# Twelve adaLN modulation products in groups of four weight slots, nine groups of them issued in the first mixer

## The reference

```python
cs = jax.nn.silu(c)                                   # (1, 1024)
for i in range(DEPTH):                                # 2 layers
    mod = (cs @ ada_w[i] + ada_b[i])[:, None, :]      # 1024 x 6144 weights each
    sh1, sc1, gt1, sh2, sc2, gt2 = jnp.split(mod, 6, axis=-1)
    h = rmsnorm_2(x, norm_w[i, 0]) * (1.0 + sc1) + sh1
    ...
```

## Time and profile before

| | us |
|---|---|
| median of 3 runs | 3378.33 (3377.92 to 3379.85) |
| the profiled execution | 3374.32 |
| its span, first to last instruction | 3372.4 |
| TensorE busy | 3001.6 |
| DVE busy | 1308.4 |
| ACT busy | 1030.4 |
| POOL busy | 243.7 |

### The profile page before, as it was taken

One profiled execution on the slowest core, in us unless ns is written; L12 is line 12 of the kernel. 1 busy time (PEld: TensorE's weight loads), 2 busy tenths in 40 slices (PEclk: granted clock), 3 DMA queues, 4 the chain that ended last, 5 costly groups with the idle time before them and its releaser, 6 DMA issues.

```text
span 3372.4 us, 44139 instructions
## 1 busy us (share of the span) xinstructions
PE 3001.6 (89%) x18608; PEld 2286.4 (68%) x18608; DVE 1308.4 (39%) x2098; ACT 1030.4 (31%) x1734; POOL 243.7 (7%) x189
## 2 busy tenths in 40 slices
PE   8989579989887888789898999999796879999998
PEld 6878467878675777668786656565595766656564
DVE  5563466555455334355463111111284541111111
ACT  5443335454443221254443111111253241111111
POOL 1000001010001223110010000000102300000000
PEclk9999699999997999889998999999897979999999
DMA  7423015445234552045343799999450036999994
GB/s 317 188 96 138 25 70 198 183 159 188 90 138 175 212 188 76 13 175 187 110 153 151 306 379 367 380 367 379 191 178 10 14 125 258 367 379 369 377 370 200
DMA packets 95539, 695.31 MB, mean 206 GB/s; under 512 B 10592, under 2 KB 10720, under 8 KB 11232
## 3 DMA queue, kind: packets, MB, share of 16 engines
q1 hardware_dynamic: 95328, 692.32, 52.5%
HBM read 691.23 MB, written 1.05 MB: 205 GB/s over the span
## 4 chain that ended last, share of the span: by engine, by line
PE 83%; DVE 8%; ACT 5%; issue 3%; POOL 1%; DMA 0%; ACTq 0%; SPq 0%; DVEq 0%; POOLq 0%
PE bank L1451 13%; PE bank L714 11%; PE bank L716 11%; PE bank L715 11%; PE bank L1498 7%; PE bank L1514 7%; PE bank L1429 4%; PE bank L1733 2%; PE bank L1741 2%; PE bank L1745 1%; PE bank L2193 1%; PE bank L1845 1%; PE bank L543 1%; PE bank L1307 1%; PE bank L1328 1%
## 5 line engine op out<-in xcount | busy, mean ns | idle before, releaser
L1451 PE MATMUL bank<-weight_ring,packed_h 128*64 128x256 f32 x2176 | 285.4, 379 | 0.0
L714 PE MATMUL bank<-source_hi_lo,weight_hi_lo 128*128 128x256 f32 x864 | 256.0, 296 | 28.3 <-DVE source_hi_lo L704 11.9
L1507 DVE COPY down<-bank 128x512 f32<-128x512 f32 x128 | 88.5, 692 | 475.2 <-PE bank L1498 475.2
L1451 PE MATMUL bank<-more_slots,packed_h 128*64 128x256 f32 x1920 | 257.0, 379 | 1.5 <-ACT packed_h L1438 1.5
L714 PE MATMUL bank<-gate_up_hi_lo,x_hi_lo 128*128 128x512 f32 x640 | 253.9, 397 | 0.0
L715 PE MATMUL bank<-source_hi_lo,weight_hi_lo 128*128 128x256 f32 x864 | 250.2, 290 | 0.0
L716 PE MATMUL bank<-source_hi_lo,weight_hi_lo 128*128 128x256 f32 x864 | 250.1, 289 | 0.0
L716 PE MATMUL bank<-gate_up_hi_lo,x_hi_lo 128*128 128x512 f32 x640 | 249.7, 390 | 0.0
L715 PE MATMUL bank<-gate_up_hi_lo,x_hi_lo 128*128 128x512 f32 x640 | 249.1, 389 | 0.0
L1451 PEld LDWEIGHTS bank<-weight_ring,packed_h 128*64 128x64 f32 x2176 | 196.2, 137 | 74.4 <-issue 18.1
L1514 PE MATMUL bank<-down,hidden_and_scatter_T 128*128 128x512 f32 x512 | 233.8, 599 | 1.6 <-DVE down L1507 1.6
(11 more groups left out here) (520 smaller groups left out, 5527.9 us busy)
## 6 DMA issues: line engine op xcount, KB each, us to landing
weight_ring<-weight_slots SPq DMA_DIRECT2D x443, 1024.0 KB, 6.2
more_slots<-weight_slots SPq DMA_DIRECT2D x212, 1024.0 KB, 7.8
params_sb<-small_params SPq DMA_DIRECT2D x1, 3215.0 KB, 17.9
x_sb<-x_T SPq DMA_DIRECT2D x1, 1024.0 KB, 5.0
out_T<-x_sb SPq DMA_DIRECT2D x4, 256.0 KB, 2.1
params_sb<-small_params SPq DMA_DIRECT2D x1, 73.5 KB, 4.8
```

Source lines behind the costliest of these rows:

```text
L714: e.matmul(out, w[0], x[0], start=start, stop=False, skip_group_check=shared)
L1451: mm = e.matmul(ps[x * CAP:(x + 1) * CAP, m * FB:(m + 1) * FB], self.hc[:, c, (2 * (p % 2) + x) * CAP:(2 * (p % 2) + x + 1) * CAP], wt[:, ...
L1507: e.tensor_copy(self.out[p % 2][:, m * 512:(m + 1) * 512], k.banks.at(n, "down", p, m)[:, :]).then_inc(*k.up("expert_out", n, p, m))
```

## The change

The weights' layout puts 36 of the 48 modulation slots between the attention's: 24 behind the two compression slots, then the first slot of the output product, 12 more modulation slots, and the other five of the output product. 12 slots stay where all 48 were, in `Rwkv`.

`Modulation` now has 12 groups of four slots. Group g has four steps (t = 4g + s); a step multiplies chunks 2s and 2s + 1 of each of the four slots, slot j in column group j. So each slot gets its own PSUM partitions of bank 2, nothing has to be added up, and one row copy per group (step 3 on ACT) and two column products with a 0/1 matrix of four columns (`first_of_32`; ahead of step 1 of the next group, into bank 3) serve four slots. DVE adds the bias of each group on its own (step 1 of the next group), and the gains at the end of each layer. The first product of a group waits for all four of its slots and for the row copy of the group before.

The steps are issued at these places, on TensorE, ACT and DVE alike: attention q = 0: 3 in `cmp_scores`, 4 before pair step (0,2), 1 before (0,3), 2 before (1,3); q = 1: 3, then 5 before (0,2), 2 before (0,3), 1 before (1,3), 3 before (2,3); SSD: 1 before each step 2, 4 after the sums; `Rwkv`: 5, 5 and 4 ahead of the blocks, and none in them.

```diff
-    pk.add("one_32nd", np.full((P, 1), 1 / 32, np.float32))
+    pk.add("first_of_32", (i[:, None] == 32 * np.arange(4)[None, :]).astype(np.float32))
@@ lay_out
-            by_rows(np.concatenate([wo[h * 64:h * 64 + 64] for h in pair] + [wo[512:]], 0))
+            wo = np.concatenate([wo[h * 64:h * 64 + 64] for h in pair] + [wo[512:]], 0)
+            ada = np.concatenate([a["ada_w_2"][i] for i in range(2)], 1)
+            by_columns(ada[:, :6 * D])
+            by_rows(wo[:FB])
+            by_columns(ada[:, 6 * D:9 * D])
+            by_rows(wo[FB:])
...
-            for i in range(2):
-                by_columns(a["ada_w_2"][i])
+            by_columns(a["ada_w_2"][1][:, 3 * D:])
@@ Modulation
+    def plan(self, groups):
+        k = self.k
+        for g in range(len(self.slots), len(self.slots) + groups):
+            taken = [k.weights.take() for _ in range(4)]
+            self.slots.append([(i, k.weights.mem(i)) for i in taken])
+            for i in taken:
+                k.weights.done(i, ("mod_product", g))
...
+    def step_pe(self, e, g, s):
         k = self.k
+        if s == 1 and g:
+            self.columns_pe(e, g - 1)
+        if g == self.GROUPS:
+            return
+        if s == 0:
+            e.wait_ge(*(k.ge("mod_row", g - 1) if g else k.ge("silu_c")))
+            for i, _ in self.slots[g]:
+                e.wait_ge(*k.weights.landed(i))
+        for c in (2 * s, 2 * s + 1):
+            for j, (_, w) in enumerate(self.slots[g]):
+                mm = e.matmul(k.bank[2][32 * j:32 * j + 32, 0:FB], k.cs[:, c:c + 1].to_broadcast([P, 32]), w[:, c * FB:(c + 1) * FB],
+                              start=c == 0, stop=c == C - 1, skip_group_check=True)
+        if s == 3:
+            mm.then_inc(*k.up("mod_product", g))
+
+    def columns_pe(self, e, g):
         k = self.k
+        e.wait_ge(*k.ge("mod_row", g))
+        if g:
+            e.wait_ge(*k.ge("mod_added", g - 1))
+        for fc in range(2):
+            mm = e.matmul(k.bank[3][:, fc:8:2], k.mod_rows[:, g % 2, fc * P:(fc + 1) * P], k.par("first_of_32"), start=True, stop=True)
+        mm.then_inc(*k.up("mod_column", g))
+
+    def step_act(self, e, g, s):
+        k = self.k
+        if s == 3 and g < self.GROUPS:
+            if g >= 2:
+                e.wait_ge(*k.ge("mod_column", g - 2))
+            e.wait_ge(*k.ge("mod_product", g))
+            e.activation(k.mod_rows[:, g % 2, :], k.bank[2][:, 0:FB], ACT.Copy).then_inc(*k.up("mod_row", g))
+
+    def step_dve(self, e, g, s):
+        if s != 1 or g == 0:
+            return
...
+        e.wait_ge(*k.ge("mod_column", g - 1))
+        e.tensor_tensor(part(r), k.bank[3][:, 0:C], k.par(f"ada_b{i}")[:, r * C:(r + 1) * C], ALU.add).then_inc(*k.up("mod_added", g - 1))
@@ Rwkv, on PE, ACT and DVE alike
-        self.mod.fill(e, "PE", 5)
+        k.modulation.fill(e, "PE", 5)
         self.heads_pe(e, "kk", self.xx, ("kk_squared", n), "kk_sums")
-        self.mod.fill(e, "PE", 5)
+        k.modulation.fill(e, "PE", 5)
         self.heads_pe(e, "bonus", self.xx, ("rk_scaled", n, C - 1), "bonus")
-        self.mod.fill(e, "PE", 2)
+        k.modulation.fill(e, "PE", 4)
...
         for s in range(inv[0].steps):
-            self.mod.fill(e, "PE", 1)
...
         for j in (2 * q, 2 * q + 1):
-            self.mod.fill(e, "PE", 2)
@@ NsaSsd, on PE, ACT and DVE alike
+    BESIDE = ({(0, 2): 4, (0, 3): 1, (1, 3): 2}, {(0, 2): 5, (0, 3): 2, (1, 3): 1, (2, 3): 3})
...
+        k.modulation.fill(e, "PE", 3)
...
             for j, step in self.pair_steps(q):
+                k.modulation.fill(e, "PE", self.BESIDE[q].get((j, step), 0))
                 self.pair_pe(e, q, j, step)
...
         for x, step in self.four_steps():
+            k.modulation.fill(e, "PE", int(step == 2))
             self.four_pe(e, x, step)
```

More of the change, by code:

```diff
@@ L1798, with __init__ @@
 class Modulation:
[L1802 to L1810, removed]
+    GROUPS, LAYER = 12, 6
+    def __init__(self, k):
+        self.k, self.slots, self.written = k, [], {}
+    def plan(self, groups):
[5 more added lines that the diff above has]
+                k.weights.done(i, ("mod_product", g))
@@ L1812, in restart, with fill @@
     def restart(self):
         self.written = {}
-    def fill(self, e, engine, pieces):
+    def fill(self, e, engine, steps):
         done = self.written.get(engine, 0)
-        for p in range(done, min(done + pieces, 2 * self.SLOTS + 1)):
+        self.written[engine] = min(done + steps, 4 * self.GROUPS + 2)
+        for t in range(done, self.written[engine]):
             if engine == "PE":
[L1819 to L1824, removed]
@@ L2016, in act @@
         gs, kk, t3, t4 = self.m0, self.m1, self.xx, k.y
-        self.mod.fill(e, "ACT", 5)
+        k.modulation.fill(e, "ACT", 5)
         e.wait_ge(*k.ge("sum_before", n))
@@ L2030, in act @@
         e.activation(al(t3), al(gs), ACT.Exp, scale=-self.KAPPA).then_inc(*k.up("decay", n))
-        self.mod.fill(e, "ACT", 2)
+        k.modulation.fill(e, "ACT", 4)
         for sg in range(2):
@@ L2034, in act @@
                 self.block_act(e, sg, q)
-        self.mod.fill(e, "ACT", 99)
         d, sq = self.sg, self.a
@@ L2072, in dve @@
         sg, a, r, v, kx = self.sg, self.a, self.r, self.v, self.kk_
-        self.mod.fill(e, "DVE", 5)
+        k.modulation.fill(e, "DVE", 5)
         e.wait_ge(*k.ge("rkv", n, 23))
@@ L2102, in dve @@
         e.tensor_tensor(al(kx), al(kx), al(t4), ALU.mult).then_inc(*k.up("K", n))
-        self.mod.fill(e, "DVE", 2)
+        k.modulation.fill(e, "DVE", 4)
         e.wait_ge(*k.ge("decay", n))
@@ L2109, in dve @@
                 self.block_dve(e, sg_, q)
-        self.mod.fill(e, "DVE", 99)
         d, sq, y = self.sg, self.a, k.y
@@ L2265, in block_act @@
         for s in range(inv[0].steps):
-            self.mod.fill(e, "ACT", 1)
             for v in inv:
@@ L2298, in block_dve @@
         for s in range(inv[0].steps):
-            self.mod.fill(e, "DVE", 1)
             for v in inv:
@@ L2588, in cmp_scores_act @@
         e.activation(self.pc[:, :, :], self.pc[:, :, :], ACT.Exp, scale=self.SCALE).then_inc(*k.up("cmp_exp", n, q))
+        k.modulation.fill(e, "ACT", 3)
         for m in range(2):
@@ L2621, in cmp_scores_dve @@
         e.tensor_tensor(pc[:, :, :], pc[:, :, :], bc(sc), ALU.mult).then_inc(*k.up("cmp_probs", n, q, 6))
+        k.modulation.fill(e, "DVE", 3)
     def pair_steps(self, q):
@@ L2721, in attention_act @@
             for j, step in self.pair_steps(q):
+                k.modulation.fill(e, "ACT", self.BESIDE[q].get((j, step), 0))
                 self.pair_act(e, q, j, step)
@@ L2729, in attention_dve @@
             for j, step in self.pair_steps(q):
+                k.modulation.fill(e, "DVE", self.BESIDE[q].get((j, step), 0))
                 self.pair_dve(e, q, j, step)
@@ L2858, in ssd_act @@
         for x, step in self.four_steps():
+            k.modulation.fill(e, "ACT", int(step == 2))
             self.four_act(e, x, step)
@@ L2891, in ssd_dve @@
         for x, step in self.four_steps():
+            k.modulation.fill(e, "DVE", int(step == 2))
             self.four_dve(e, x, step)
```

68 lines of the change are left out of this document (27 added, 41 removed).

## The result

The changed kernel takes 3389.61 us (median; 3385.23 to 3393.64), the kernel before 3378.77 beside it. The ratio is 1.0032, 95% interval 1.002 to 1.0045: slower by 0.32%, or 10.8 us. The prediction said slower by 22.5. The sign and the cause hold; the price of the attention stage was too high.

A forecast was written before the change was run, and what follows sets the result against it. TensorE, busy 89% of the span with 83% of the chain, was taken to bound the kernel. Blocks -42, preparation +10.5, attention +44 and state-space part +10 gave +22.5 us, say 3401 us; range 3366 to 3415.

The forecast's parts named there:

- The refill: TensorE's stop between groups while two slots load, some 7.4 us; five in the attention, 37 us, 9 covered: 28.
- the attention's own work and slots: TensorE in the attention: own work 42.5 us, 24 slots at 1.7 = 41, near the half clock.
- +44: The attention's growth in us, taken between +26 (slots at full clock) and +49 (slots at 1.7 us).
- The half clock: TensorE's granted clock stayed at 0.50 from 1067 to 1081 with slots running; the attention's slots were costed near it.
- Rival 2: Added products hold the attention's clock near 0.9 and its own work shrinks: attention +12, total -14.5, 3364 us; chance 0.13.
- The row copies: In the attention, some 3 us where ACT's or DVE's step still ends last.
- The blocks: RWKV blocks, with all 36 slots that lay in them gone: 42 us saved, bounds 38 and 48.
- The preparation: RWKV stage ahead of the blocks, where DVE waits three times for a column step: +10.5 us, bounds 5 and 13.
- The first wait: In the preparation, DVE waits for a product and a column step before its scans: +1.3 us.
- the second: In the preparation, DVE waits for group 10's column step behind step 44's refill: +8.9 us including the first wait.
- the third: In the preparation, the last column step waits for ACT's row copy: L2105 2.2 us later, 0.6 back on TensorE.
- The state-space part: Its 12 steps: 2 us remaining from eight single steps, 5 for refill 27/28, 3 at the reciprocal; +10, bounds 6 and 14.

The follow-up runs named there:

- the run that takes it out: The kernel after, with the RWKV stage's fills at 5, 4 and 5 steps instead of 5, 5 and 4: 3382.52 us, ratio to before 1.0014.
- one slot per step: The kernel after with weights laid out anew, so each step waits for one slot and frees it; same bytes, loads and products: 3356.00 us, ratio to before 0.9938.
- without any loads: The kernel after, the nine groups ahead of the RWKV stage multiplying by the residual stream instead of loaded slots: 5758.16 us, with modulation values not the right ones.
- 8 added calls a step: The kernel before plus 8 unread product calls at each of the 24 attention places, without loads or waits: 3376.55 us, ratio to before 0.9996.
- two banks: The one slot per step kernel with alternating product banks, column step and addition two steps later, and RWKV fills moved: 3347.69 us, ratio to before 0.9914.
- (16): The kernel before plus 16 unread product calls at each of the 24 attention places: 3383.50 us, ratio to before 1.0015.
- (32): The kernel before plus 32 unread product calls at each of the 24 attention places: 3423.34 us, ratio to before 1.0138.

## Why the prediction was off in size

- **The refill** was right in its mechanism, its place and its length: 7.4 us forecast, 7.38 ahead of step 4 and 7.45 ahead of step 12, 7.39 and 7.57 in the preparation. Ahead of steps 8 and 20, where I let 4 and 5 us of it be covered, 5.2 and 3.9 us were left instead of 3.4 and 2.4. Together TensorE stood 31.6 us at the five places of the attention, where the forecast had 28. Taking the refills away gave 27.7. That this is so near 28 is luck, since 15.9 of it is idle time and 11.8 is the clock, which the forecast booked elsewhere.
- **The failed step is the attention's own work and slots, taken at fixed prices.** I wrote: own work 42.5, 24 slots at 1.7 = 41, column steps 5. They measured 33.6, 35.3 and 4.2, 15.4 us less together; the waits measured 34.0 where I had 28 + 3. That makes 12.4 less than the +48.5 of my sum, and 7.9 less than the +44 that I took between +26 and +49. The 42.5 us were read at a granted clock of 0.63, and I added work to the stage while I kept the clock. The half clock came from one stretch, 1067 to 1081 in the earlier trace rows; why the clock stayed at 0.50 there and went higher in the attention no run shows. Rival 2 had the right mechanism, the own work that shrinks with the clock, but only at a clock of about 0.9, and I gave it 0.13; no other case of mine let the own work shrink. The clock went part of the way, to 0.70. With the refills gone it reached 0.82 and 0.86. Those kernels are faster than before, but rival 2 kept the refills in its sum, so they don't confirm its 3364.
- **The row copies** were in the sum at 3 us. With one slot per step the attention's whole price is 8.4, and a second bank and a later column step remove all of it (tried together, not one by one). In the kernel after the copies lie beside the refills: the one wait put down to a copy, 7.7 us ahead of step 16, covers a refill too. Its four loads were issued from 413.26 on. At step 12 the product began 7.39 us after such an issue; by that the weights would be there at 420.65 (an estimate), and the copy ended at 420.81. So the 8.4 us that stayed with one slot per step are not a sum of slots' time, but this wait come to light.
- **The blocks**: 42 forecast, 42.9 measured. The difference between a block with and without slots in one trace was a good price, half clock at its end included.
- **The preparation**: 10.5 forecast, 8.6 measured. The first wait +1.2, the second 7.0 (7.1 by the run that takes it out), the third +1.1 instead of 2.2, and 0.7 back on TensorE.
- **The state-space part**: 10 forecast, 9.0 measured; 0.6 is left with one slot per step, but 4.0 without any loads, at a lower clock. So the refill of steps 27/28 (5.80 us ahead of the product) and what hangs on it are worth 5.0 to 8.4 here, against my 5, and the eight single steps with the last column step 0.6 to 4.0, against my 5. In the output product no wait for a load appears, as said.
- **The stages ahead of the attention and between the mixers** moved by +2.2 and -2.2 and cancelled. I had no term for that. The first is not `silu(c)`, which the change moves there: the kernel before with 8 added calls a step lacks that move and is 2.5 us late at the same place.

By these entries the forecast errs by 7.9 in the attention, 1.0, 1.9 and 0.9 in the other three: 11.7 in all, less the 0.3 behind the blocks, which is the difference between 22.5 and 11.1.

## What to carry to other kernels

When work is moved into a stage where TensorE waits at a low granted clock, the stage's own busy time is not a constant: cost it at both levels of the clock, own work included. Look at how many places of a ring come free at once before looking at how much there is to load: here the order of the bytes within four slots was worth 33.6 us. A copy that another engine makes for moved work stands in that engine's order, so give it a second buffer and a later reader, and look what else stands behind that reader: in the state-space part the late reader cost 2.3 us.

## What the runs showed that I had not expected

Work that nobody reads can be free, or even pay. With 384 added instructions the attention took 69.6 us at a clock of 0.88, instead of 71 at 0.63, a difference that one execution of each can't tell from none. With 352 added instructions in the waits of the RWKV stage the kernel gained 12.7 us, which is clear of noise.

On this the Trainium skill, "TensorE: Matmul & The Clock Gate", Part 1, What's actually happening, says that the throttled state is the default and activity releases it; the added products in the earlier trace rows's stretch agree, as the clock there rose from 0.63 to 0.88.

The profiled executions of kernels that are alike in a stage differ in it by several us. Take the stretch between DVE's first reciprocal of the state-space part and the last r/k/v product. The kernel after gained 2.2 us on before in it and that with one slot per step 2.1, while that with two banks lost 3.0. The three kernels with added products have the very instructions of before there, and they moved by -1.6 (8 calls), +0.2 (16) and -4.0 (32). TensorE's busy time in that stretch goes with it: 527 us in before, 523 in the shortest, 531 in the longest. The granted clock there is 0.95, 0.96 and 0.94; what decides it is open. A few us in a stage that is not touched are no evidence for or against an edit.
